# Sparse attention on one core: each head's values made once from the latent keys, instead of a value product behind every sum over keys

## What is computed

```
q_lat = rmsnorm(h @ w_dq); q = (q_lat @ w_uq)      # 16 heads x 128
kv = rmsnorm(h @ w_dkv)                            # one latent key of 128 per token
score = sum over 16 index heads of relu(q_idx . k_idx) * w_idx, causal
sel = top 128 keys of score
logits = q . kv[sel] * 128**-0.5 + bias[head, distance]
p = softmax(logits)
o_lat = p @ kv[sel]                                # per head: 128 wide
o = o_lat @ w_uv[head]                             # 128 -> 64 per head
x += concat(o) @ w_o
```

## Time and profile before

| | before |
|---|---|
| runs, us | 2277.31, 2284.5, 2481.31 (median 2284.5) |
| profiled execution: span, us | 2277.6 |
| PE busy | 2186.2 us, 96% |
| DVE, ACT, POOL busy | 55%, 32%, 2% |
| mean granted clock of TensorE | 0.971 of full |
| chain that ended last, by engine | PE 85%, DVE 9%, DMA 3%, ACT 1% |

### The profile page before, as it was taken

How to read it: one execution, slowest core, us unless ns; L and a number is a source line. 1 busy time by engine, 2 the same in 40 slices (tenths; PEclk the granted TensorE clock), 3 DMA queues, 4 the chain that set the end, 5 groups by cost and what they waited for, 6 DMA issues and landing times.

```text
span 2277.6 us, 28155 instructions
## 1 busy us (share of the span) xinstructions
PE 2186.2 (96%) x10212; PEld 1790.3 (79%) x10212; DVE 1243.8 (55%) x2008; ACT 726.5 (32%) x998; POOL 49.4 (2%) x87
## 2 busy tenths in 40 slices
PE   6996999999999989999999999999998999999998
PEld 5885888788878778888888888888765778888886
DVE  6532535588547888535446544435558535535345
ACT  3221223433424543222224222223355653222222
POOL 0000000000000000000000000000001210000000
PEclk8998999999999999999999999999887999999999
DMA  4339333331125316333323333333210003333321
GB/s 141 92 105 135 102 101 83 93 83 47 57 73 131 87 53 187 99 102 92 101 84 102 102 92 93 101 98 87 75 58 1 1 23 99 92 94 100 101 82 67
DMA packets 362749, 200.23 MB, mean 88 GB/s; under 512 B 13507, under 2 KB 356678, under 8 KB 362662
## 3 DMA queue, kind: packets, MB, share of 16 engines
q1 hardware_dynamic: 359238, 184.73, 28.3%
q0 software_dynamic: 3424, 14.35, 3.7%
HBM read 191.55 MB, written 7.37 MB: 87 GB/s over the span
## 4 chain that ended last, share of the span: by engine, by line
PE 85%; DVE 9%; DMA 3%; issue 1%; ACT 1%; SPq 1%; DVEq 0%; ACTq 0%
PE ps L1381 24%; PE ps L1382 24%; PE ps L1383 24%; DMA w_raw<-in_ffn_w_gate 2%; PE ps L1754 2%; PE ps L1776 1%; PE ps L1503 1%; DVE index_scores L1273 1%; DVE w_lo L735 1%; PE ps L1400 1%; PE ps L1402 1%; PE ps L1401 1%; PE ps L1745 1%; DVE stat L1256 1%; DVE index_scores L1258 1%
## 5 line engine op out<-in xcount | busy, mean ns | idle before, releaser
L445 ACT ACTIVATE w_hi<-w_raw 128x1024 fp32r<-128x1024 f32 x351 | 371.7, 1060 | 1120.6 <-PE ps L1383 1051.5
L1381 PE MATMUL ps<-h_hi,w_hi 128*128 128x512 f32 x1704 | 669.4, 393 | 21.5 <-DVE silu_gate L854 18.6
L1382 PE MATMUL ps<-h_lo,w_hi 128*128 128x512 f32 x1704 | 665.8, 391 | 0.0
L1383 PE MATMUL ps<-h_hi,w_lo 128*128 128x512 f32 x1704 | 665.6, 391 | 0.0
L735 DVE TENSOR_TENSOR w_lo<-w_raw,w_hi 128x1024 fp32r<-128x1024 f32 x351 | 428.9, 1222 | 338.1 <-ACT w_hi L445 338.0
L1381 PEld LDWEIGHTS ps<-h_hi,w_hi 128*128 128x128 f32 x1704 | 321.7, 189 | 90.2 <-DVE w_lo L735 21.8
L1383 PEld LDWEIGHTS ps<-h_hi,w_lo 128*128 128x128 f32 x1704 | 321.5, 189 | 67.5
L1382 PEld LDWEIGHTS ps<-h_lo,w_hi 128*128 128x128 f32 x1704 | 321.9, 189 | 66.1
L1381 PE MATMUL ps<-act_hi,w_hi 128*128 128x512 f32 x704 | 273.9, 389 | 0.0
L1382 PE MATMUL ps<-act_lo,w_hi 128*128 128x512 f32 x704 | 273.9, 389 | 0.0
L1383 PE MATMUL ps<-act_hi,w_lo 128*128 128x512 f32 x704 | 273.9, 389 | 0.0
(11 more groups left out here) (273 smaller groups left out, 2068.2 us busy)
## 6 DMA issues: line engine op xcount, KB each, us to landing
w_raw<-in_ffn_w_gate SPq DMA_DIRECT2D x88, 512.0 KB, 3.9
w_raw<-in_ffn_w_up SPq DMA_DIRECT2D x88, 512.0 KB, 3.8
w_raw<-in_ffn_w_down SPq DMA_DIRECT2D x64, 512.0 KB, 3.9
w_raw<-in_hy_w_in SPq DMA_DIRECT2D x44, 512.0 KB, 3.8
w_raw<-in_ffn_w_down SPq DMA_DIRECT2D x32, 384.0 KB, 3.5
w_raw<-in_hy_w_out SPq DMA_DIRECT2D x16, 512.0 KB, 4.1
line_scratch<-line POOLq DMA_DIRECT2D x1, 5120.0 KB, 55.0
acum_rows<-acum_scratch POOLq DMA_DIRECT2D x4, 1024.0 KB, 10.8
```

The costliest lines, as they stand in the source:

```text
L445: act.activation(w_hi[:, s, :], w_raw[:, s, :], ACT.Copy).then_inc(hi_ready, 1)
L1381: pe.matmul(ps[:, bank, :], wh, rh[:, k, :], start=k == 0, stop=False)
L1382: pe.matmul(ps[:, bank, :], wh, rl[:, k, :], start=False, stop=False)
L1383: mm = pe.matmul(ps[:, bank, :], wl, rh[:, k, :], start=False, stop=k == nk - 1)
```

## The change

The latent keys times every head's value matrix are made once. For each of four blocks of 128 keys and each half of the heads, one product (stationary: 128 columns of `kvT`; moving: 8 heads x 64 columns of `w_uv_sb`, 512 columns) gives `head_values[2 * block + half]`, token on the partitions. The eight products stand among the index rows, one after every sixth, in banks 4 to 7; ACT copies the first four to SBUF after rows 5, 11, 17 and 23, and the other four after row 47 (they go to the `sq` buffers, which are free once DVE has added the last index row). `weighted` takes the place of `latent`: the stationary operand is now a head's 64 columns of `head_values`, the result the head's output, 64 partitions high, put directly into the half of the bank that `values` wrote before. `values`, `latent_out`, `o_latent`, `kvtok`, its four transposes and its copy are gone. ACT takes out a bank of eight heads as before, now straight after the sums. The engines' other work, and DVE's whole queue, are unchanged.

```diff
-        kvtok = at("kvtok", [P, TT, AL], 34)
...
-        o_latent = nc.alloc_sbuf_tensor_at("o_latent", [P, 2, TOK], F32, offset=H0 + 26 * KB)
+        head_values = [nc.alloc_sbuf_tensor_at(f"head_values{j}", [P, 8 * AV], F32, offset=H0 + (26 + 2 * j) * KB)[:, :] for j in range(3)]
+        head_values.append(at("head_values3", [P, 8 * AV], 34)[:, :])
+        head_values += [sq[:, j, :] for j in range(4)]
...
-                    if t == 11:
-                        act.wait_ge(d_tr, 2)
-                        act.activation(kvtok[:, :, :], ps[:, 0, :].rearrange("p (c d) -> p c d", c=TT), ACT.Copy).then_inc(d_trev, 1)
+                def head_values_out(j):
+                    act.wait_ge(v_mm, j + 1)
+                    if j == 4:
+                        act.wait_ge(d_acc, (TT - 1) * IH)
+                    act.activation(head_values[j], ps[:, 4 + j % 4, :], ACT.Copy).then_inc(v_out_sb, 1)
...
+                    if r % 6 == 5 and r < 24:
+                        head_values_out(r // 6)
...
-                def latent_out(g):
-                    act.wait_ge(a_pv, 4 * g + 4)
-                    if g >= 2:
-                        act.wait_ge(a_uv, g - 1)
-                    act.activation(o_latent[:, g % 2, :], ps[:, 4 + g % 2, :], ACT.Copy).then_inc(a_ol, 1)
...
+                for j in range(4, 8):
+                    head_values_out(j)
...
-                    if u == 1:
-
+                def head_values_mm(j):
+                    if j == 0:
                         pe.wait_ge(d_kv, 1)
-                        for c in range(TT):
-                            mm = pe.transpose(ps[:, 0, c * P:(c + 1) * P], kvT[:, c * P:(c + 1) * P], ident[:, :])
-                        mm.then_inc(d_tr, 1)
+                        pe.wait_ge(uv_landed, 16)
+                        pe.wait_ge(tile_out, T1 + 4 + 4 + KT + AH)
+                    if j >= 4:
+                        pe.wait_ge(v_out_sb, j - 3)
+                    pe.matmul(ps[:, 4 + j % 4, :], kvT[:, (j // 2) * P:(j // 2 + 1) * P],
+                              w_uv_sb[:, 8 * (j % 2):8 * (j % 2) + 8, :].rearrange("p h d -> p (h d)"), start=True, stop=True).then_inc(v_mm, 1)
...
+                    if r % 6 == 5:
+                        head_values_mm(r // 6)
...
-                def latent(r):
-                    b, g = r // AH, r // 4
+                def weighted(r):
+                    b, h = r // AH, r % AH
+                    m = h // 2
+                    if r == 0:
+                        pe.wait_ge(v_out_sb, 8)
+                    if h % 8 == 0 and b:
+                        pe.wait_ge(a_o, 2 * (b - 1) + h // 8 + 1)
                     pe.wait_ge(a_pt, r + 1)
-                    if r % 4 == 0 and g >= 2:
-                        pe.wait_ge(a_ol, g - 1)
                     for st in range(b + 1):
-                        mm = pe.matmul(ps[:, 4 + g % 2, (r % 4) * P:(r % 4 + 1) * P], kvtok[:, st, :], probs_T[:, r % 2, st * P:(st + 1) * P],
-                                       start=st == 0, stop=st == b, skip_group_check=True)
+                        mm = pe.matmul(ps[(h % 2) * AV:(h % 2 + 1) * AV, 6 + m // 4, (m % 4) * P:(m % 4 + 1) * P],
+                                       head_values[2 * st + h // 8][:, (h % 8) * AV:(h % 8 + 1) * AV],
+                                       probs_T[:, r % 2, st * P:(st + 1) * P], start=st == 0, stop=st == b, skip_group_check=True)
                     mm.then_inc(a_pv, 1)
-
-                def values(g):
...
```

More of the change, by code:

```diff
@@ L269, in build_program @@
         d_tile, d_ix, d_relu, d_acc = sem("d_tile"), sem("d_ix"), sem("d_relu"), sem("d_acc")
-        a_log, a_max, a_exp, a_rec, a_nrm, a_tr, a_pt, a_pv, a_ol, a_uv, a_o = (sem("a_" + n) for n in (
-            "log", "max", "exp", "rec", "nrm", "tr", "probs_T", "pv", "ol", "uv", "o"))
+        a_log, a_max, a_exp, a_rec, a_nrm, a_tr, a_pt, a_pv, a_o = (sem("a_" + n) for n in (
+            "log", "max", "exp", "rec", "nrm", "tr", "probs_T", "pv", "o"))
+        v_mm, v_out_sb = sem("v_mm"), sem("v_out_sb")
         k_top, k_mask, k_causal = sem("k_top"), sem("k_mask"), sem("k_causal")
@@ L664, in p_out, with values_out @@
                     act.activation(probs_T[:, r % 2, 0:w], ps[:, 2 + r % 2, 0:w], ACT.Copy).then_inc(a_pt, 1)
-                def latent_out(g):
-                    act.wait_ge(a_pv, 4 * g + 4)
-                    if g >= 2:
-                        act.wait_ge(a_uv, g - 1)
-                    act.activation(o_latent[:, g % 2, :], ps[:, 4 + g % 2, :], ACT.Copy).then_inc(a_ol, 1)
-                def values_out(g):
-                    act.wait_ge(a_uv, g + 1)
-                    b, half = g // 4, (g % 4) // 2
+                def values_out(k):
+                    b, half = k // 2, k % 2
+                    act.wait_ge(a_pv, 8 * k + 8)
                     act.activation(att_out[:, 4 * half:4 * half + 4, b * P:(b + 1) * P],
                                    ps[:, 6 + half, :].rearrange("p (m t) -> p m t", m=4), ACT.Copy).then_inc(a_o, 1)
+                for j in range(4, 8):
+                    head_values_out(j)
                 for r in range(NR + LAG + 4):
@@ L688, in mix1 @@
                         p_out(r - LAG)
[L689 to L692, removed]
+                    if r >= LAG + 2 and (r - LAG - 2) % 8 == 7:
+                        values_out((r - LAG - 2) // 8)
                     if EARLY <= r < EARLY + KT:
@@ L1733, in mix1 @@
                     pe.matmul(ps[:, r % 4, 0:w], index_q[R, h // 2, b * P:(b + 1) * P], index_k[R, 0:w], start=True, stop=True).then_inc(d_ix, 1)
+                    if r % 6 == 5:
+                        head_values_mm(r // 6)
                 pe.wait_ge(d_relu, (TT - 1) * IH)
-                pe.wait_ge(tile_out, T1 + 4 + 4 + KT + AH)
-                pe.wait_ge(uv_landed, 16)
                 NR = TT * AH
@@ L1780, in mix1 @@
                     if LAG + 1 <= r < NR + LAG + 1:
-                        latent(r - LAG - 1)
-                    if r >= LAG + 3 and (r - LAG - 3) % 4 == 3 and (r - LAG - 3) // 4 < NR // 4:
-                        values((r - LAG - 3) // 4)
+                        weighted(r - LAG - 1)
                 n0 = n + NU["mix1"] - KT
```

## The result

The changed kernel is slower by a quarter of a per cent: median 2286.03 us over 12 runs, against 2279.99 us of the kernel before over its 12. The ratio of the runs is 1.0027, 95% interval 1.0018 to 1.0035, so +4 to +8 us; the one slow run of the kernel before, 2481.31 us, is not in it. The forecast was 2285 us (range 2270 to 2297), from a loss worked out as 3.8 us.

A forecast was written before the change was run, and what follows sets the result against it. DVE bounds the index rows, DVE and PE the first attention rows, PE blocks 2 and 3. Terms -0.4 + 0.3 + 0.3 + 0 + 3.6 = +3.8 us give 2281.4 (span) or 2288.3 (median); forecast midway, 2285 us, range 2270 to 2297.

The forecast's parts named there:

- What bounds it, and the price in the group: Attention rows: PE bounds blocks 2 and 3; a value group costs 0.78 us, 0.34 of it for changing width and back.
- Transposes, -0.4: Four transposes at 1654 us go, on a PE without pause there: -0.4 us.
- Index rows, +0.3: Eight products of 512 columns among the index rows, where DVE is the bound: +0.3 us, bounds 0 and +2.
- Hand-over, +0.3: From index rows to attention: ACT copies four banks after row 47, delaying the first exp; +0.3 us, bounds 0 and +1.
- the first exp then waits 0.9: Hand-over: ACT's copies last to about 1733.6 us, while the first exp ran at 1732.70 before, so it waits 0.9 us.
- Blocks 0 and 1, 0: First attention blocks, eight rounds of four rows at -0.4 to +0.6 us each: bounds -3 and +5, taken 0.
- a clock of 1.00 from block 1 on: Attention rows, a sign that the forecast holds: PE's granted clock is full from block 1 on.
- Rival C: Attention rows: gaps and half-width sums lower the clock to 1.2 GHz, total slower by over 2%, up to 2369 us; chance 0.03.
- Blocks 2 and 3, +3.6: Last attention blocks: +10.4 us from mode changes in 32 rows, -5.5 for seven value groups, -1.35 at the tail.
- the forecast's -1.35 and -0.5: Tail: -1.35 us as ACT's copy and value products go, -0.5 as the last two rows lack full-width work between.
- The rule on which the case hung: PE: a mode change drains the engine, a tile change doesn't; so 0.34 us is two drains, in each of 64 rows.
- The rival by which narrow weights, with their shorter load, would shorten the sums: Attention sums: if bound by weight loads, narrow ones take half of 0.67 us; given no chance of its own.

The follow-up runs named there:

- wide sums: The changed kernel with sums 128 wide, a pair of heads' values as stationary operand and half of each result thrown away; 2273.88 us, ratio 0.9966.
- pairs: The changed kernel with the sums of an even and an odd row made together, in alternating halves of the array; 2269.01 us, ratio 0.9945.
- early exp: One exp of one element ahead of ACT's four late copies; in the changed kernel 2286.26 us, with two rows' sums together 2268.83 us.
- four buffers: Two rows' sums together, with four buffers of transposed probabilities instead of two and sums one turn later; 2256.61 us, ratio 0.9901.
- warm start: Four products of 512 columns after the last index row; in the changed kernel 2286.87 us, with paired sums and four buffers 2257.86 us.
- wide touch: The kernel before plus one product 128 wide and 16 columns long ahead of each row's logits; 2289.65 us, ratio 1.0043.
- narrow touch: The kernel before plus one product 64 wide and 16 columns long ahead of each row's logits; 2298.14 us, ratio 1.0078.
- wide sums with narrow touch: The changed kernel with 128-wide sums, plus one product 64 wide and 16 columns long ahead of each row's logits; 2295.67 us, ratio 1.0074.

## Why the prediction held, and where it did not

The time fell in the range and the direction was right. That it came out about 1 us from the forecast is luck, in two ways. The forecast stood on runs whose median was 2284.5 us, and the kernel before turned out to run at 2279.99; the change itself was +6 where +3.8 was worked out. And in the stretch errors of both signs met.

- **What bounds it, and the price in the group** (0.34 us for a way into the narrow mode and back; nothing gained by narrow products one at a time). Right. Rows of 2.16 us were forecast, 2.15 came; block 3 was to have the same +0.34 on 2.42 and had +0.33. Full-width sums gave the 0.33 back (2.42 a row). The doubt that the pace of one half alone is unknown is settled: 0.11 us a record, from sums of 4, 6 and 8 records.
- **Transposes, -0.4.** No run isolates it. From the projections of the query latent to the first index add the changed kernel took 0.4 us more, not less, but it also had 1.8 us more at the low clock there.
- **Index rows, +0.3.** 0.0 in both places where the products stand there. The lower bound was right, in rows whose mean clock was 0.80.
- **Hand-over, +0.3.** It was 1.2 us, outside its bounds of 0 and +1. The failed step is "the first exp then waits 0.9": it came 1.9 us later against the first row. The four copies took 2.06 us, less than the 2.4 forecast, but the load of the exp table, which is not among the rows that the prediction shows and which ACT had done in its pause, now stood behind them.
- **Blocks 0 and 1, 0.** This step failed, outside its bounds of -3 and +5. It was +7.5 with the hand-over, 6.3 without. The sum put PE's work at 2.4 GHz; PE ran at 1.2 GHz until 28.9 us after the first row, and was the bound at 1.69 us a row in block 0. At 2.4 GHz the estimate holds: in block 1 the changed kernel's rounds of four rows, from 1764.45 to 1770.64 and so on, take 6.19 us, against 6.49 before. The sign "a clock of 1.00 from block 1 on" failed with it: the clock rose 5.1 us after PE had begun block 1. Rival C was nearest, with a low clock in the rows with narrow sums, but put it in all of them; the low clock lasted some 22 us longer than before, and that cost 6.
- **Blocks 2 and 3, +3.6.** +1.4 with the tail. The tail's -1.5 is near the forecast's -1.35 and -0.5. The rows gave 2.9 and not 5.4. Part of it is that the prediction took all 32 rows at PE's pace: before the change the chain of waits ran through DVE's extreme and selection round and ACT's exp from 1775.50 to 1779.08, in the first rows of block 2, where PE's added work had room; in the changed kernel it stays on PE there. Part is where the stretch is cut: PE's turns for rows 32 to 62 hold eight value groups and not seven, so that the prediction's own prices give +4.3 there.

The rule on which the case hung stands in the Trainium skill's "TensorEngine Tiling (Array Packing)", Key Properties: changing the mode drains the engine and changing the tile doesn't. The trace agrees in its times with both halves: 0.33 us for a mode change there and back, and none for alternating halves (16 records of a pair in 1.02 us, as 8 of one head). That the time is a drain the profile doesn't show. The rival by which narrow weights, with their shorter load, would shorten the sums did not come: a narrow product takes the 0.11 us a record that a wide one takes.

What stays open is why the clock stayed low so long. These are the times, after the first row, at which it came back, each of one profiled execution:

| rows | clock back after, us |
|---|---|
| before; with the eight products | 7.0; 10.5 |
| wide sums | 7.9 |
| pairs; with early exp; with four buffers; with these and a warm start | 11.6; 18.3; 8.3; 10.9 |
| before with wide touch; with narrow touch | 14.5; 17.3 |
| changed kernel; with early exp; with warm start | 28.9; 28.0; 24.6 |
| wide sums with narrow touch | 30.9 |

Wide against narrow sums, with hand-over and pause alike, is 7.9 against 28.9, and all executions with narrow sums one at a time lie at 24.6 or more. So such sums prolong the low clock in block 0, and neither hand-over nor pause explains it. Why they do so is not shown. The pair that differs by the narrow touch alone (7.9 and 30.9) has no control with a wide touch, and in the kernel before the wide touch alone moved the return from 7.0 to 14.5; so the share of the mode changes against that of PE's mere length of work in a row is not separated. In the four long cases the return fell 0.7 to 5.4 us after PE had begun block 1, whose logits have twice the columns; whether block 0's short rows are a condition was not tested.

## What to carry to other kernels

In float32 as here, a narrow product was no cheaper than a wide one, and between wide ones it cost a third of a microsecond: count the changes of mode and not the products. Reassociate so that narrow products of both halves stand together, or pad them to full width with the neighbour's columns and throw half away. And when a step is put in front of another function's first use on ScalarE, look where the table load goes.

## What was not expected of the hardware

- A product of 16 columns with 128-wide weights, between full-width ones, cost 0.22 us a row, two records of 0.11, as much as one of 128 columns; with 64-wide weights it cost 0.07 where the mode fitted. The Trainium skill's "TensorE: Matmul & The Clock Gate", section LDWEIGHTS, gives a load's time by its columns; the estimate from it is 107 ns for 128 columns and 53 for 64. By it the short product is bound by its load. The trace's 0.11 a record agrees for 128; for 64 it shows less, 0.07 for two records.
- With PE busy throughout by the profile, the clock stayed at 1.2 GHz for 22.90 of 22.90 us in the changed kernel, and with the touch for ten us on end twice (10.00 of 10.00 busy at 0.50). A full busy share of the profile does not mean that the clock will rise soon. With the warm start it fell from 2.4 GHz where PE was waiting, at 1.81 of 4.12 us busy.
